# Delta rule of a hybrid decoder layer: two of four pairs of heads on exchanged halves, six banks in turn, a new order on three engines

## The reference

```
sa = einsum('bhvk,bhk->bhv', S, -kk_t)
S  = S * w_t + sa * (kk_t * a_t) + v_t * k_t        # outer products over (v, k)
y  = einsum('bhvk,bhk->bhv', S, r_t)
```

## Time and profile before

| | |
|---|---|
| median of 3 runs | 3400.47 us (3394.62 to 3410.07) |
| the profiled execution | 3404.79 us |
| its span, first to last instruction | 3403.0 us |
| PE / DVE / ACT busy over the span | 94% / 58% / 35% |
| delta rule, from the first product of the third chunk to that of the samples | 780.37 to 1341.26 us, 15 turns |

### The profile page before, as it was taken

One profiled execution on the slowest core, in us unless ns is written; L12 is line 12 of the kernel. 1 busy time (PEld: TensorE's weight loads), 2 busy tenths in 40 slices (PEclk: granted clock), 3 DMA queues, 4 the chain that ended last, 5 costly groups with the idle time before them and its releaser, 6 DMA issues.

```text
span 3403.0 us, 78807 instructions
## 1 busy us (share of the span) xinstructions
PE 3209.2 (94%) x34512; PEld 3112.7 (91%) x34512; DVE 1980.2 (58%) x3819; ACT 1197.6 (35%) x2440; POOL 163.4 (5%) x169
## 2 busy tenths in 40 slices
PE   6899986869999999888999999999999999999997
PEld 6899984659999999888999999999999999999997
DVE  6567658336666665335655556555556655556465
ACT  4323333435555555333322222222222222223432
POOL 0000000001010100122000000000000000000111
PEclk8999998979999999898999999999999999999998
DMA  5344330010011000333122222222222222222222
GB/s 162 119 121 143 119 92 1 3 54 26 26 33 29 25 26 23 96 105 104 57 68 75 69 69 64 68 68 75 69 69 65 68 67 75 69 69 85 73 84 87
DMA packets 331592, 238.16 MB, mean 70 GB/s; under 512 B 16608, under 2 KB 317408, under 8 KB 331232
## 3 DMA queue, kind: packets, MB, share of 16 engines
q1 hardware_dynamic: 331248, 233.10, 23.1%
HBM read 206.51 MB, written 25.38 MB: 68 GB/s over the span
## 4 chain that ended last, share of the span: by engine, by line
PE 52%; DVE 3%; DMA 2%; issue 1%; ACT 1%; SPq 0%; DVEq 0%; ACTq 0%
PE tail_bank L1193 29%; PE tail_bank L1230 14%; PE tail_bank L1249 5%; PE tail_bank L1181 2%; DMA tail_raw<-in_w_out 2%; PE tail_bank L1262 1%; ACT tail_w_hi L840 1%; DVE tail_x L993 1%; DVE tail_xn_lo L998 0%; DVE mix_b L1005 0%; DVE tail_xn_lo L981 0%; DVE mix_b L1124 0%; DMA tail_raw<-in_w_pg 0%; DVE mix_a L1005 0%; PE tail_bank L1168 0%
## 5 line engine op out<-in xcount | busy, mean ns | idle before, releaser
L1193 PE MATMUL tail_bank<-tail_xn_hi,tail_w_hi 128*128 128x352 f32 x2112 | 682.9, 323 | 8.0 <-DVE tail_xn_lo L998 7.9
L1193 PE MATMUL tail_bank<-tail_xn_lo,tail_w_hi 128*128 128x352 f32 x2112 | 681.0, 322 | 0.0
L1193 PE MATMUL tail_bank<-tail_xn_hi,tail_w_lo 128*128 128x352 f32 x2112 | 680.9, 322 | 0.0
L1193 PEld LDWEIGHTS tail_bank<-tail_xn_hi,tail_w_hi 128*128 128x128 f32 x2112 | 397.9, 188 | 11.1 <-issue 6.7
L1193 PEld LDWEIGHTS tail_bank<-tail_xn_lo,tail_w_hi 128*128 128x128 f32 x2112 | 398.3, 189 | 0.1
L1193 PEld LDWEIGHTS tail_bank<-tail_xn_hi,tail_w_lo 128*128 128x128 f32 x2112 | 398.2, 189 | 0.0
L1230 PE MATMUL tail_bank<-tail_f_hi,tail_wd_hi 128*128 128x352 f32 x1056 | 341.7, 324 | 7.0 <-DVE mix_b L1099 2.7
L1230 PE MATMUL tail_bank<-tail_f_lo,tail_wd_hi 128*128 128x352 f32 x1056 | 339.6, 322 | 0.0
L1230 PE MATMUL tail_bank<-tail_f_hi,tail_wd_lo 128*128 128x352 f32 x1056 | 339.6, 322 | 0.0
L840 ACT CAST tail_w_hi<-tail_raw 128x1024 fp32r<-128x1024 f32 x180 | 185.3, 1045 | 400.5 <-DMA tail_raw<-in_w_gate 208.9
L976 DVE TENSOR_TENSOR tail_w_lo<-tail_raw,tail_w_hi 128x1024 fp32r<-128x1024 f32 x180 | 220.8, 1226 | 160.4 <-ACT tail_w_hi L840 160.1
(11 more groups left out here) (479 smaller groups left out, 6458.1 us busy)
## 6 DMA issues: line engine op xcount, KB each, us to landing
tail_raw<-in_w_gate SPq DMA_DIRECT2D x66, 512.0 KB, 4.0
tail_raw<-in_w_val SPq DMA_DIRECT2D x66, 512.0 KB, 4.0
tail_raw<-in_w_down SPq DMA_DIRECT2D x66, 512.0 KB, 3.3
in_raw<-in_w_in SPq DMA_DIRECT2D x54, 512.0 KB, 4.2
in_xs<-in_xT SPq DMA_DIRECT2D x12, 1408.0 KB, 6.8
scratch_zr<-in_zo SPq DMA_DIRECT2D x84, 176.0 KB, 1.9
rw_z<-scratch_zr SPq DMA_DIRECT2D x16, 896.0 KB, 5.5
tail_raw<-in_w_out SPq DMA_DIRECT2D x24, 512.0 KB, 4.5
```

The source lines that it names most:

```text
L1193: mm = pe.matmul(out[:, 0:TW], l, r, start=(k == 0 and j == 0), stop=(k == KD - 1 and j == 2))
```

## The change

The operands of pairs `j` = 2 and 3 can lie "natural" (`NAT`, as before) or "exchanged" (`SWP`: the head of partitions 0 to 63 lies on 64 to 127 and the other way). A product that takes natural operands and leaves an exchanged result, or the reverse, runs pairs 0 and 1 on the diagonal quarters and pairs 2 and 3 on the two others, in the order `j` = 0, 2, 1, 3. Where operands and result lie alike, all four pairs are on the diagonal, as before. The result of a product on four quarters takes two neighbouring banks (`TWO_BANKS`: pairs 0 and 1 in one, 2 and 3 in the next), any other one bank.

- On four quarters: `AabT`, `Aab`, `AqbT`, `AakT`, `AqkT`, `Bt`, `Kt`, `Vt`, `X`, `Z32`, `X32t`, `Z64`, `X64t`, one term of `RH`, both of `S`, two of three of `Y`: 18 of a chunk's 30.
- On two quarters: `D2`, `Dt2`, `D4`, `Dt4`, `D8`, `X2`, `X3`, `X4`, `X32`, `U`, the other term of `RH` (`RH+`) and of `Y` (`Y+`): 12 of 30.

`RH+` and `Y+` open their banks; the terms that follow on other quarters wait for the semaphore `opened`, that is for the opening products' end. The six banks are one ring, taken in the order in which PE meets the products of both chunks (`bank_places`); a product waits for the copies of the last users of its one or two banks (`wait_bank_free`). What was one tile in turn for several results (`D8`, `Kt`, `Bt`, `X`, `Vt`, `RH`, `U`) gets a tile each, `yt` gets two. The masks are stored twice as wide (13 x 128 columns), so that the load of them from memory doubles. The orders of PE, DVE and ACT are three new lists for each half; the sample chunk follows PE's list for `q` = 0, with its end rewritten in the same manner.

```diff
+PE_HALF = [("RH+ RH Aab AabT w U AqbT D2 Dt2 AakT X2 D4 Y+ Dt4 Y Bt D8 X3 S Vt X4 Kt Z32 X centred X32t X32 AqkT Z64 ss X64t "
+            "squares").split(),
+           ("AabT Kt Aab RH+ RH AakT Dt2 D2 spread AqbT X2 D4 Dt4 Bt kinv X3 D8 U Y+ X4 Vt Y bonus Z32 X S X32t X32 AqkT Z64 g "
+            "X64t").split()]
+DVE_HALF = ["DO Dt Xt AqbT hat_k AakT hat_b X2 L X3 Sadd X4 S t X32t X32 AqkT hat_a sg X64t".split(),
+            "kp Dt DO y_inv Xt AakT inv AqbT y_scale X2 y_bonus y_gate X3 kkn hat_a b X4 bonus Sadd X32t X32 AqkT hat_b S X64t hat_k".split()]
+ACT_HALF = ["th RH kk2 hat_v U D2 Dt2 wt D4 Dt4 Y Bt D8 at Vt Kt Z32 X y_centre Z64 nrm y_root".split(),
+            "Kt RH hat_v decays Dt2 D2 e D4 Dt4 Bt D8 U Y Vt Z32 X bb Z64 g".split()]
...
-NBANK = 3
+NBANK = 6
...
-        masks = e.sb("masks", [P, NMASK * C])
+        masks = e.sb("masks", [P, NMASK, 2 * C])
...
-        wide = [[e.ps(f"bank{q}{i}", [P, Q, HP, C]) for i in range(NBANK)] for q in range(Q)]
-        bank = [[b[:, 0] for b in row] for row in wide]
+        ring = e.ps("ring", [P, NBANK, HP * P])
...
-                    for j in range(HP):
-                        for n, (l, r) in enumerate(operands):
-                            for h in HALF:
-                                by = ident[h] if transpose else r[h, j, :]
-                                last = pe.matmul(out[h, j, :], l[h, j, :], by, start=(n == 0), stop=(n == len(operands) - 1))
-                    last.then_inc(mm[q], 1)
...
+                def rows(j, h, swapped):
+
+                    return HALF[1 - h if swapped and j >= 2 else h]
...
+                def product(b, out, terms, opens=True, closes=True):
+
+                    alone = opens and closes and len(terms) == 1
+                    for n, (l, r, side_in) in enumerate(terms):
+                        for j in (0, 2, 1, 3):
+                            for h in range(2):
+                                on, to = rows(j, h, side_in), rows(j, h, out)
+                                at_bank, cols = place(b, j)
+                                by = ident[on] if r is None else r[on, j, :]
+                                last = pe.matmul(ring[to, at_bank, cols], l[on, j, :], by, start=alone or (opens and n == 0 and j % 2 == 0),
+                                                 stop=alone or (closes and n == len(terms) - 1 and j % 2 == 1))
+                                if not closes and j == 3:
+                                    last.then_inc(opened, 1)
+                    return last
...
+                        last = product(b, SWP, [(m["bT"], m["aT"], NAT)])
...
+                        last = product(b, SWP, [(m["Dt"], m["D"], SWP)])
...
+                    if stage == "RH+":
+                        wait_made(q, t, "AakT", "Vt")
+                        open_bank(b, SWP, (m["AakT"], m["Vt"], SWP))
+                        return
...
+                    if stage in OPENED:
+                        wait_for(opened, turns["opened"])
```

More of the change, by code:

```diff
@@ L1282 @@
 PREP_POOL = ["rk"]
[L1283 to L1290, removed]
@@ new lines @@
+WITH_STATE, OPENED = ["RH", "U", "S", "Y"], ["RH", "Y", "Zs"]
+INTRA = ["AabT", "Aab", "AqbT", "AakT", "AqkT", "D2", "Dt2", "D4", "Dt4", "D8", "X2", "X3", "X4", "X", "Bt", "Kt", "Vt", "Z32", "X32t", "X32",
+         "Z64", "X64t"]
+ONE_BANK = ["D2", "Dt2", "D4", "Dt4", "X2", "D8", "X3", "X4", "X32", "U", "RHs"]
+TWO_BANKS = [s for s in INTRA + WITH_STATE + ["Zs"] if s not in ONE_BANK]
+NBANK = 6
+DVE_INTRA, DVE_STATE = ["Dt", "Xt", "DO", "AqbT", "AakT", "X2", "X3", "X4", "X32t", "X32", "AqkT", "X64t"], ["Sadd", "S"]
@@ L1294, with bank_places @@
 POST_DVE = ["inv", "dn", "dbonus", "y"]
-NBANK = 3
+def bank_places(half):
+    first, n = {}, 0
+    for s in (s.rstrip("+") for s in half if s not in OPENED):
+        if s in ONE_BANK + TWO_BANKS:
+            if s in TWO_BANKS and n % NBANK == NBANK - 1:
+                n += 1
+            first[s] = n
+            n += 1 if s in ONE_BANK else 2
+    return first, -(-n // NBANK) * NBANK
 NMASK = 13
@@ L1609, in copy_out @@
-                def copy_out(q, t, stage):
-                    m, smp = M[q], is_samples(t)
[L1612 to L1622, removed]
-                        first = SD if smp else MD
[L1624 to L1638, removed]
-                        dve.wait_ge(dve_out[q], at(t, DVE_OUT, "Sadd"))
@@ L1942, in prepare @@
                             last.then_inc(prep_pe, 1)
[L1944 to L1963 removed]
+                had = {}
@@ L2010, in intra @@
+                        last = product(b, SWP, [(m["X"], m["Z32"], NAT)])
                     elif stage == "X32":
-                        product(q, t, stage, [(m["Z"], m["X"])])
+                        wait_made(q, t, "X", "Z32")
+                        last = product(b, NAT, [(m["Z32"], m["X"], NAT)])
                     elif stage == "Z64":
-                        product(q, t, stage, [(m["O64"], m["Xt"])], after=["X32t"])
-                    elif stage == "X64t":
-                        product(q, t, stage, [(m["X"], m["Z"])], after=["X32", "Z64"])
+                        wait_made(q, t, "O64", "X32t")
@@ new lines, in samples, with states @@
+                    last.then_inc(smp_pe, 1)
+                def states(p, half, terms, first):
+                    for i in range(2):
+                        for j in (0, 2, 1, 3):
+                            for h in range(2):
+                                on, to = rows(j, h, SWP), rows(j, h, NAT)
+                                t = (2 * i + j % 2) * C
+                                last = pe.matmul(ring[to, state_banks(p)[j // 2], t:t + C], half[on, j, :], terms[2 * p + i][on, j, :],
+                                                 start=first and i == 0 and j % 2 == 0, stop=not first and i == 1 and j % 2 == 1)
+                    return last
@@ new lines, in _ @@
+                finish(NB - 1, 2)
+                wait_for(opened, turns["opened"] + 2)
+                pe.wait_ge(smp_act, 3)
+                for n, (l, r) in enumerate(((m["U"], m["AqbT"]), (m["Vt"], m["AqkT"]))):
+                    for j in (0, 2, 1, 3):
+                        for h in range(2):
+                            on, to = rows(j, h, SWP), rows(j, h, NAT)
+                            at_bank, cols = place(smp_y, j)
+                            last = pe.matmul(ring[to, at_bank, cols], l[on, j, :], r[on, j, :], start=False, stop=(n == 1 and j % 2 == 1))
```

561 lines of the change are left out of this document (338 added, 223 removed).

## The result

The changed kernel takes 3347.12 us (median of 4 runs, 3344.82 to 3349.62) against 3401.9 for the kernel before beside it: a ratio of 0.9841 (95% interval 0.9819 to 0.9863), faster by 1.6%. The prediction was 3265 with a range from 3246 to 3318. Of the 135 us that it saw, 55 came.

What follows compares the result with a forecast made beforehand. PE was taken to set the stage's pace. Fifteen turns falling from 37.39 to 29.0 us (125.9), + 5.6 + 5.0 - 1.4, gave 135 us off 3404.8, 3270; the median, 4.3 lower, 3265; range 3246 to 3318.

Steps and rivals of the forecast that it cites:

- Price of a product: On PE, a product was to take 0.233 us on four quarters and 0.467 us on two.
- the two rules: Trainium skill: row tiles cannot access one PSUM bank at the same time; matmul starts lie at least some 25 ns apart.
- PE's sum of 26.8 us a turn: PE's work in a turn of two halves: twice 9.8 us of products plus 7.2 us of other steps.
- Waits that were walked: Four places in PE's new lists, followed, where PE waits over 0.1 us; together 1.5 us a turn.
- The fourth: At `RH+` in the half for `q` = 1, PE waits 0.25 us for banks that `AabT` has just filled.
- I take 2.2: All PE waits of a turn taken as 2.2 us, range 1.6 to 3.4, giving a turn of 29.0 us.
- Rival 3: PE's issue of instructions bounds four-quarter products at 0.40 us, saving only 40 us in 33 halves: 3361 us; chance 0.04.
- the earlier trace: Step `w` for the samples before the change: 30 of 32 four-quarter instructions start within 0.41 us, 14.6 ns each.
- Two first halves: The two halves before the steady stretch were to save 2.0 and 3.6 us, together 5.6 (3 to 7).
- Samples: The sample chunk after the steady stretch was to save 5.0 us of 6.1 (0 to 8).
- Masks: Loading another 416 KB of masks ahead of DVE's first instruction was to cost 1.4 us.

Runs made afterwards that it cites:

- e4: The changed kernel with 120 four-quarter, 80 two-quarter and 80 whole-array products that wait for nothing put ahead of the stage, run once for its trace: 3513.97 us.
- e1: The changed kernel with every product on two quarters, its order, ring of banks and two-bank results kept: 3382.11 us, ratio 0.9950 to the kernel before.
- e3: The changed kernel with AqbT, AqkT, Bt and Kt each given as two matmuls of 32 columns instead of one of 64: 3412.27 us, ratio 1.0032.
- e6: The changed kernel with AabT, AqbT, Bt merged into one 192-column product and AakT, AqkT, Kt into another, lists adjusted: 3326.78 us, ratio 0.9791.
- e5: The changed kernel with the load of z cut to a few bytes from the third turn on: 3335.11 us, ratio 0.9810.

## Why the prediction was wrong

**Price of a product.** Right: 0.233 and 0.467. Here, too, two row halves write each bank of a four-quarter product and its 16 starts take 0.23 us, 14.6 ns each, so that the two rules that the prediction set against the trace do not show in this one. PE's sum of 26.8 us a turn stands.

**Waits that were walked.** Right in place and size: `RH` 0.27 us behind `RH+` (1010.51 to 1011.25, less 0.47; 0.23 was predicted), `Z32` 0.58 (1020.25 to 1021.06, less 0.23; 0.48), `X32t` 0.32 behind `S` (1006.21 to 1006.76, less 0.23; 0.3). The fourth, `RH+` for `q` = 1, is 0.29 from the last start of `Aab` (median of the 15 turns; 0.25). Two-bank copies last 0.42 on DVE, as assumed:

```profile
L1695 DVE TENSOR_TENSOR rw_AqbT<-rw_ring,rw_masks 128x256 f32<-128x256 f32 x30 | 12.7, 422 | 8.3 <-PE rw_ring L2091 7.6
```

**"I take 2.2", the sum of a turn's waits.** This is the step that failed. It held what PE waits for by semaphores and took PE's instructions as given: "PE's instructions stay equal in number" was written down as if it cost nothing. 8.6 packets of them a turn (129 / 15) at 3.81 us, the rate of e4, are 32.8 us, above the 29.0 of the forecast and above the whole of its range for a turn, 28.4 to 30.2. Of the missing 34.08 - 29.0 = 5.1 us the stops inside products make 4.5 a turn by my count (68 us in 15 turns), 3.2 by the "issue" rows above, which count only from the modelled end of the instruction before. The gaps over 0.25 us between two products come to 2.4 a turn (36 us in 95 places; some may be stops that happen to fall there), close to the 2.2 that were taken. Some 0.4 us a turn is not assigned. As to the stops, e1 shows that they go with the faster products, e3 that they grow with the number of instructions, e4 that they need nothing else.

**Rival 3** named "PE's issue of instructions" with a chance of 0.04 and a time of 3361. That its time came near is luck: it expected every start to be late, and the starts are 14.6 ns apart until a run is used up. Its remark that a dense stream could find the queue less well filled names what happened, but no cost was worked out from it. It was put aside with the earlier trace rows, 32 matmuls, a quarter of a run. So short a burst says nothing of the supply: in e4 a whole run of 128 matmuls goes through without a stop.

**The rest.** Two first halves: 5.8 us for 5.6. (The 3.6 there for the second is not "as the others do": 18 x 0.233 = 4.2.) Samples: 3.2 for 5.0; the granted clock there is 0.87 where it was 0.96, which may be the difference and was not tried. Masks: DVE's first instruction waits 13.50 us instead of 12.61, +0.9 for +1.4:

```profile
722.11 0.17 DVE L1604 TENSOR_SCALAR rw_kah<-rw_k_a 128x4 f32<-128x4 f32 x1 [13.50 <-DMA rw_lnx_b<-in_lnx_b]
```

From there to the first product it is 19.67 us instead of 21.59, 1.9 gained that nobody had counted. With 49.7 from the turns these make 49.7 + 5.8 + 3.2 + 1.9 - 0.9 = 59.7 of the span's 60.0; the stage began 2.3 us earlier and the tail took 2.1 longer, which cancel.

## What to carry to other kernels

Before PE's instructions are made shorter, divide the stage's time by the packets of PE's instruction queue. Here the kernel before stood at 4.35 us a packet and the supply at 3.8, so by estimate 129 packets left some 70 of its 561 us to win, whatever the products cost. Past that point fewer, wider instructions helped (e6), and quieter transfers a little (e5); it has to be looked at whether those that are merged away had filled waits.

## What was not expected of the hardware

- PE runs 256 instructions, then can stand still until the next 256 have come: 3.45 to 4.00 us from one run to the next, 3.81 on average in a stream without any wait (e4). Advanced Engine Details and Errata of the Trainium skill, section ISA Cache, has 16 KB as a cache line, which is 256 instructions; the packets of 16.4 KB and the runs of 128 matmuls with 128 weight loads agree.
- "issue" in PE's rows, inside a product, is such a stop: 1.8 us in the turns of the kernel before, 45.1 in those of the changed one, 67.4 with 12% more instructions.
- A float32 matmul instruction on 128 by 128 with 64 columns starts every 112 ns (e4); two of 64 by 64 on the diagonal quarters take 58 ns together, four on all quarters as well (e4, and 1005.98 to 1006.21 above).
